# Mean squares with the squares stationary and one moving column, in a one-core decoder step

## The chip, the core and the metric

The kernel runs on one core of a Trainium2 chip. Its engines have a queue each: TensorE (PE; its weight loads are PEld in the profile), VectorE (DVE), ScalarE (ACT), GpSimdE (POOL) and SyncE (SP), which issues the DMAs. They meet at semaphores. The metric is the device time of one execution in microseconds (us); lower is better.

## The reference

One layer of a hybrid decoder for 1088 tokens, 1024 of a prompt and 8 x 8 of a sample. All weights and data are float32.

```
h = rmsnorm(x, norm1_g)                            # D_MODEL = 1024
z = h @ w_in                                       # [c_q 384 | c_kv 256 | k_rope 32 | u 512 | v 512]
c_kv = rmsnorm(c_kv, kv_norm_g); q = rmsnorm(c_q, q_norm_g) @ w_q_up
a = attention(q, c_kv, k_rope) @ w_uv              # 8 heads
g = u * (w_spatial @ layernorm(v) + b)
x = x + [rmsnorm(a, out_norm_mla_g) ; rmsnorm(g, out_norm_gmlp_g)] @ w_out
h2 = rmsnorm(x, norm2_g)
x = x + (silu(h2 @ w_gate) * (h2 @ w_up)) @ w_down
y = rmsnorm(x, final_norm_g)

def rmsnorm(x, g): return x * rsqrt(mean(x * x, axis=-1) + EPS) * g
```

## The kernel before

Activations lie transposed: features on the 128 partitions, tokens along the free dimension. A product in higher precision takes three matmuls, high by high, high by low and low by high part (`mm3`, L871; its three lines L873, L874 and L875 are in most rows of the profile). A mean of squares runs across partitions, so PE computes it.

Five norms go by that route. Their parts are numbered by j: norm 1 over x (`J_N1`, L51) in four parts of 128, 256, 384 and 320 tokens (`CH1`, L49), with 8 row tiles of squares; norm 2 over c_q (3 row tiles) and c_kv (2) in three parts each of 384, 384 and 320 tokens (`CH`, L47); norm 3 over the attention output (4 row tiles), three parts; norm 4 over x after the attention (8 row tiles, which POOL has added up so that two are left), three parts; norm 5 over the output, in another division.

For each part of norms 1 to 4 this happens:

1. ACT squares x (L1429, for norm 4 L1697 too) and counts `nm_sq`.
2. PE sums: `sum_squares` (L877, matmul L881) or, for norm 4, `sum_x2` (L1265, matmul L1271). A 128 x 128 matrix of ones is stationary, the squares move, and every partition of the PSUM bank gets the sum of each token. It counts `nm_sum`.
3. DVE turns this into one value per partition: `columns` (L1892) multiplies each block of 128 tokens by the identity (L1900; for a part of 320 tokens the last 128 go by L1904), adds along the free dimension (L1908) and makes the mean (L1910). It counts `nm_mean`.
4. POOL raises to -0.5 (`power`, L674, L677).
5. DVE builds diagonal matrices of the factors (`diagonals`, L1913, L1919).
6. PE spreads them over the partitions: `spread` (L885, L889), ones times the diagonals.
7. DVE, or ACT and DVE, multiply x by the result.

Norm 5 is summed otherwise, and the change doesn't touch it: `token_sums` (L1352, L1356) has the squares stationary and one column of ones moving, so that each token's sum lands on its own partition, and L2474 makes the mean out of PSUM.

Every engine follows the order in which its block of the program is written. On PE the sums and spreads stand between products: in the first stage, for v (nine token tiles t of 24 matmuls of 512 columns each), the order is sum 0, spread 0, half of t = 0, sum 1, the other half, spread 1, sum 2, t = 1, spread 2, sum 3, t = 2, t = 3, spread 3, t = 4 and so on (L902 to L929). DVE's order there is norm 1 part 0, weight splits, parts 1 and 2, statistics of tiles 0 and 1, part 3, then the statistics and normalisation of the other tiles (L1949 to L1982). SP loads x in four parts and waits for a weight split before the third (L480 to L485). In the stage of c_q and c_kv PE has 18 products of 24 matmuls, with sums and spreads at the places of L986 and L987. In the stage of norm 3 they stand between the samples' scores and products (L1232 to L1262), in that of norm 4 between the last products of `w_out` and the first of the gate (L1275 to L1300).

Of the kernel before, what the change touches and what calls it, by code (L numbers as in the profile page):

```python
# [22 lines left out]
ALU = mybir.AluOpType  # L23
ACT = mybir.ActivationFunctionType
AX = mybir.AxisListType

P = 128
D = 1024
# [16 lines left out]
EPS = 1e-6  # L45
SCALE = QK ** -0.5
CH = [(0, 384), (384, 384), (768, 320)]  # L47
# [6 lines left out]
J_N4 = J_N3 + NC  # L54
# [45 lines left out]
def offsets(n):  # L100

    return [*range(0, n - P + 1, P)] + ([n - P] if n % P else [])
# [28 lines left out]
def build(nc, d):  # L131
    ctx = ExitStack()
    with ctx:
# [14 lines left out]
        small = Region((nc.sbuf_base + 63) // 64 * 64)  # L148
        ident = small.put("ident", [P, P])
        ones = small.put("ones", [P, P])  # L150
        diag = small.put("diag", [P, 3, P])
# [4 lines left out]
        pages = small.put("pages", [1, NB * PAGES], I32)  # L156
        mhalf = small.put("mhalf", [P, 1])
        stat6, mv = small.put("stat6", [P, 2, 6]), small.put("mv", [P, 2, 2])
        sums = small.put("sums", [P, 3])
        ms, rt = small.put("ms", [P, 4, 3]), small.put("rt", [P, 4, 3])  # L160
        ve, rv, ssq = (small.put(n, [P, 4]) for n in ("ve", "rv", "ssq"))
        mx, nmx, sm, rsm = (small.put(n, [P, 4]) for n in ("mx", "nmx", "sm", "rsm"))
# [17 lines left out]
        reg = Region(W0, R0)  # L180
# [5 lines left out]
        reg = Region(W0, R0)  # L186
# [5 lines left out]
        reg = Region(A0, B0)  # L192
        hH, hL = reg.put("hH", [P, KD, T], F32R), reg.put("hL", [P, KD, T], F32R)

        reg = Region(B0, C0)
# [10 lines left out]
        reg = Region(C0, W0)  # L206
# [4 lines left out]
        reg = Region(B0, C0 - 4 * KG * T)  # L211
# [8 lines left out]
        reg = Region(C0, W0)  # L220
# [5 lines left out]
        reg = Region(A0, B0)  # L226
# [11 lines left out]
        reg = Region(rope0, KR0)  # L238
# [8 lines left out]
        reg = Region(B0, PT0)  # L247
# [4 lines left out]
        reg = Region(PT0, PT1)  # L252
# [6 lines left out]
        reg = Region(A0, B0)  # L259
# [4 lines left out]
        reg = Region(B0, C0)  # L264
# [3 lines left out]
        wraw = reg.put("wraw", [P, 4, 1024])  # L268
        reg = Region(B0 + 2 * 16 * HALF * 2, B0 + 3 * 16 * HALF * 2)
        sq2 = reg.put("sq2", [P, 3, T])  # L270
        picked = reg.put("picked", [P, 3, P])
        reg = Region(A0, B0)
        for j in range(3, PROD):
            xH[j], xL[j] = reg.put(f"x{j}H", [P, KH, HALF], F32R), reg.put(f"x{j}L", [P, KH, HALF], F32R)
# [3 lines left out]
        reg = Region(V0, nc.sbuf_usable_end)  # L278
# [5 lines left out]
        reg = Region(B0, C0)  # L284
        ab = [reg.put(f"ab{b}", [P, TURNS, HALF]) for b in range(2)]
        reg = Region(A0, B0)
# [9 lines left out]
        reg = Region(A0 + 4 * TURNS * HALF, A0 + 8 * TURNS * HALF)  # L296
# [4 lines left out]
        reg = Region(V0, V0 + 8192)  # L301
# [3 lines left out]
        ps = ctx.enter_context(nc.psum_tensor("ps", [P, 8, 512], F32))  # L305
# [5 lines left out]
        def sem(name):  # L311
            return ctx.enter_context(nc.semaphore(name))
# [10 lines left out]
            sem(n) for n in ("made", "made_r", "made_z", "sp_masked", "split_seen", "split_hi", "split_lo"))  # L323

        nm_sq, nm_sum, nm_pick, nm_column, nm_mean, nm_pow, nm_diag, nm_spread = (
            sem("nm_" + n) for n in ("sq", "sum", "pick", "column", "mean", "pow", "diag", "spread"))

        n1_x, n1_hi, n1_lo = (sem("n1_" + n) for n in ("x", "hi", "lo"))

# [539 lines left out]
        def _(pe):  # L870
# [6 lines left out]
            def sum_squares(j, bank, sq, k, n):  # L877

                pe.wait_ge(nm_sq, j + 1)
                for kk in range(k):  # L880
                    last = nc.tensor.matmul(ps[:, bank, 0:n], ones[:, :], sq[:, kk, 0:n], start=kk == 0,  # L881
                                            stop=kk == k - 1)
                last.then_inc(nm_sum, 1)

            def spread(j, bank, n):  # L885
# [19 lines left out]
            for t in range(NT):  # L905
# [10 lines left out]
                for k in range(KD):  # L916
# [4 lines left out]
                    if (c := {0: 0, 1: 1, 3: 2, 6: 3}.get(t)) is not None:  # L921

                        pe.wait_ge(n1_lo, KD * c + k + 1)
                    last = mm3(ps[0:m, b, :], hH[:, k, cols], hL[:, k, cols], vwH[:, k, :], vwL[:, k, :],
                               k == 0, k == KD - 1)
# [60 lines left out]
            sums = {9: (0,), 10: (1,), 11: (2,), 15: (3, 4), 16: (5,)}  # L986
# [236 lines left out]
            for u in range(UNITS):  # L1223
                p = u // 4
# [40 lines left out]
            def sum_x2(c):  # L1265

                c0, n = CH[c]
                pe.wait_ge(n4_added, KD - 2)
                pe.wait_ge(nm_sq, J_N4 + c + 1)
                for i in range(2):  # L1270
                    last = nc.tensor.matmul(ps[:, 4 + c, 0:n], ones[:, :], sq2[:, 2 * i, c0:c0 + n],  # L1271
                                            start=i == 0, stop=i == 1)
                last.then_inc(nm_sum, 1)

            for m in range(KD):  # L1275
# [611 lines left out]
        def _(dve):  # L1887
# [1 line left out]

                return nc.vector.scalar_tensor_tensor(out, x, gain, factor, ALU.mult, ALU.mult)  # L1890

            def columns(j, bank, width, n, picked=diag):  # L1892

                full, k = n // P, len(offsets(n))
                dve.wait_ge(nm_sum, j + 1)
                if j:
                    dve.wait_ge(nm_mean, j)
                    if picked is diag:
                        dve.wait_ge(nm_spread, j)
                last = nc.vector.tensor_tensor(picked[:, 0:full, :],  # L1900
                                               ps[:, bank, 0:full * P].rearrange("p (i n) -> p i n", n=P),
                                               ident[:, :].unsqueeze(1).broadcast_to((P, full, P)), ALU.mult)
                if k > full:
                    last = nc.vector.tensor_tensor(picked[:, full, :], ps[:, bank, n - P:n], ident[:, :],  # L1904
                                                   ALU.mult)
                last.then_inc(nm_pick, 1)
                dve.wait_ge(nm_pick, j + 1)
                nc.vector.tensor_reduce(sums[:, 0:k], picked[:, 0:k, :], AX.X, ALU.add).then_inc(nm_column, 1)  # L1908
                dve.wait_ge(nm_column, j + 1)
                nc.vector.tensor_scalar(ms[:, j % 4, 0:k], sums[:, 0:k], 1.0 / width, EPS,  # L1910
                                        ALU.mult, ALU.add).then_inc(nm_mean, 1)

            def diagonals(j, n):  # L1913
# [316 lines left out]

            def columns4(c):

                columns(J_N4 + c, 4 + c, D, CH[c][1], picked)

            def weight_sums(i):
# [418 lines left out]
```

## Time and profile before

| | us |
|---|---|
| three runs, median | 1470.52 |
| lowest and highest of them | 1469.29, 1474.88 |
| the profiled execution | 1473.64 |
| span of the profiled execution | 1471.7 |

| engine | busy us | share of the span | instructions |
|---|---|---|---|
| PE | 1354.1 | 92% | 9216 |
| PEld | 1259.0 | 86% | 9216 |
| DVE | 827.0 | 56% | 1304 |
| ACT | 506.6 | 34% | 870 |
| POOL | 439.4 | 30% | 278 |

### The profile page before, as it was taken

How to read it: one execution, taken by the hardware profiler on the slowest of the kernel's cores; microseconds unless marked ns; L12 is line 12 of the kernel's file. 1: busy time of each engine (PE TensorE's matmuls, PEld its weight loads, DVE VectorE, ACT ScalarE, POOL GpSimd, SP SyncE). 2: the span in 40 equal slices, each digit the busy share in tenths (PEclk: the TensorE clock that was granted, in tenths of full speed). 3: DMA queues.
4: the chain of work that ended last, by engine and by line, in shares of the span. 5: the costliest groups of instructions: out<-in, count | busy, mean ns of one | idle time of the engine just before them, and what ended most of it. 6: DMA issues, size and time to landing. Idle time of an engine off the chain costs nothing.

```text
span 1471.7 us, 23463 instructions
## 1 busy us (share of the span) xinstructions
PE 1354.1 (92%) x9216; PEld 1259.0 (86%) x9216; DVE 827.0 (56%) x1304; ACT 506.6 (34%) x870; POOL 439.4 (30%) x278
## 2 busy tenths in 40 slices
PE   6979998799999898999669999999999989999987
PEld 4758898688888765899659999999999989999987
DVE  4793114666666432514765454434445547989975
ACT  3412212455655431301332222222222224444452
POOL 1161222434333202154644444444444410000000
PEclk9989999899999899999779999999999999999998
DMA  7011010200003532442012222222222249766503
GB/s 230 3 46 59 25 34 4 70 1 19 1 15 117 188 115 112 163 141 94 4 37 74 74 88 80 73 80 76 69 73 73 88 159 368 266 194 229 196 1 122
DMA packets 64376, 142.10 MB, mean 97 GB/s; under 512 B 7490, under 2 KB 14530, under 8 KB 63586
## 3 DMA queue, kind: packets, MB, share of 16 engines
q1 hardware_dynamic: 64290, 140.93, 28.1%
q8 instruction: 57, 0.93, 0.3%
q14 instruction: 29, 0.24, 0.1%
HBM read 118.35 MB, written 22.55 MB: 96 GB/s over the span
## 4 chain that ended last, share of the span: by engine, by line
PE 71%; DVE 15%; issue 4%; DMA 4%; POOL 2%; ACT 2%; SPq 0%; DVEq 0%; POOLq 0%; ACTq 0%
PE ps L873 21%; PE ps L874 21%; PE ps L875 21%; DMA araw<-in_w_dn 2%; PE ps L1096 2%; PE ps L881 2%; DVE x L1890 2%; PE ps L1159 1%; DVE aHL L2442 1%; DMA x<-in_x 1%; DVE bHL L2445 1%; PE ps L1202 1%; DVE mx L2113 1%; DVE bsum L2434 1%; DVE mL L2227 1%
## 5 line engine op out<-in xcount | busy, mean ns | idle before, releaser
L827 POOL TENSOR_TENSOR ws<-wraw,ws 128x1024 fp32r<-128x1024 f32 x55 | 136.5, 2483 | 199.9 <-ACT ws L1425 199.9
L873 PE MATMUL ps<-bHL,aHL 128*128 128x272 f32 x616 | 180.2, 293 | 11.5 <-DVE bHL L2445 11.5
L875 PE MATMUL ps<-bHL,aHL 128*128 128x272 f32 x616 | 179.0, 291 | 0.0
L874 PE MATMUL ps<-bHL,aHL 128*128 128x272 f32 x616 | 178.8, 290 | 0.0
L873 PEld LDWEIGHTS ps<-bHL,aHL 128*128 128x128 f32 x616 | 117.8, 191 | 13.0 <-DVE bHL L2445 13.0
L2308 DVE TENSOR_TENSOR bufP<-bufP,ps 128x544 f32<-128x544 f32 x66 | 47.5, 721 | 139.3 <-PE ps L875 137.1
L1425 ACT ACTIVATE ws<-wraw 128x1024 fp32r<-128x1024 f32 x55 | 58.3, 1061 | 181.9 <-PE ps L875 181.9
L874 PEld LDWEIGHTS ps<-bHL,aHL 128*128 128x128 f32 x616 | 117.8, 191 | 0.0
L875 PEld LDWEIGHTS ps<-bHL,aHL 128*128 128x128 f32 x616 | 117.6, 191 | 0.0
L827 POOL TENSOR_TENSOR ws<-wsum,ws 128x1024 fp32r<-128x1024 f32 x22 | 64.8, 2946 | 66.2 <-ACT ws L1425 66.2
L865 POOL TENSOR_TENSOR rt<-ms,mhalf 128x3 f32<-128x3 f32 (+1 forms) x3 | 3.1, 1039 | 265.3 <-DVE ms L2474 265.3
L2129 DVE TENSOR_TENSOR pTL<-ps,pTH 128x512 fp32r<-128x512 f32 (+1 forms) x96 | 53.1, 554 | 46.3 <-ACT pTH L1425 44.8
L782 POOL TENSOR_TENSOR prob<-prob,rsm 128x128 f32<-128x128 f32 (+5 forms) x48 | 49.7, 1042 | 96.7 <-DVE rsm L2102 96.7
L2308 DVE TENSOR_TENSOR bufC<-bufP,ps 128x544 f32<-128x544 f32 x42 | 30.3, 720 | 80.3 <-PE ps L875 72.9
L1425 ACT ACTIVATE aHL<-araw 128x512 fp32r<-128x512 f32 x66 | 41.7, 631 | 89.1 <-DVE araw L2417 59.9
L1425 ACT ACTIVATE pTH<-ps 128x512 fp32r<-128x512 f32 (+1 forms) x96 | 46.9, 490 | 52.1 <-PE ps L1096 51.1
L1096 PE MATMUL ps<-ident,prob 128*128 128x128 f32 x288 | 54.2, 295 | 11.5 <-DVE prob L2107 7.4
L873 PE MATMUL ps<-x4H,ws 128*128 128x272 f32 x176 | 52.3, 297 | 7.4 <-POOL x4L L832 7.4
L873 PE MATMUL ps<-x3H,ws 128*128 128x272 f32 x176 | 51.8, 294 | 6.9 <-DVE x3L L2278 6.9
L1578 ACT ACTIVATE prob<-ps,nmx 128x128 f32<-128x128 f32 (+3 forms) x64 | 47.4, 741 | 28.9 <-DVE nmx L2116 28.9
L873 PE MATMUL ps<-x1H,ws 128*128 128x272 f32 x176 | 52.2, 297 | 5.2 <-POOL x1L L832 5.2
L2113 DVE TENSOR_REDUCE mx<-ps 128x1 f32<-128x128 f32 (+3 forms) x64 | 48.1, 751 | 12.5 <-PE ps L1077 12.2
(356 smaller groups left out, 4509.9 us busy)
## 6 DMA issues: line engine op xcount, KB each, us to landing
araw<-in_w_dn SPq DMA_DIRECT2D x121, 256.0 KB, 3.3
wraw<-in_w_gu SPq DMA_DIRECT2D x44, 512.0 KB, 3.6
cp<-in_cache SPq DMA_DIRECT2D x64, 272.0 KB, 4.7
ab<-acts SPq DMA_DIRECT2D x34, 272.0 KB, 4.9
acts<-bufC SPq DMA_DIRECT2D x22, 272.0 KB, 2.1
x<-in_x SPq DMA_DIRECT2D x4, 1088.0 KB, 8.1
x2s<-x SPq DMA_DIRECT2D x8, 544.0 KB, 9.2
x<-x2s SPq DMA_DIRECT2D x8, 544.0 KB, 6.2
```

Of the source, the lines that this page charges most:

```text
L782: pool.tensor_tensor(row, row, rsm[:, r % 4:r % 4 + 1].broadcast_to((P, n)), ALU.mult).then_inc(s_pn, 1)
L827: pool.tensor_tensor(w[:, 1, :], w_source(j), w[:, 0, :], ALU.subtract).then_inc(cw_lo, 1)
L873: nc.tensor.matmul(out, wh, xh, start=start, stop=False)
L874: nc.tensor.matmul(out, wh, xl, start=False, stop=False)
L875: return nc.tensor.matmul(out, wl, xh, start=False, stop=stop)
L881: last = nc.tensor.matmul(ps[:, bank, 0:n], ones[:, :], sq[:, kk, 0:n], start=kk == 0, stop=kk == k - 1)
L1096: last = nc.tensor.transpose(ps[:, 4 + x % 2, P * qi:P * qi + P], prob[:, at:at + P], ident[:, :])
L1425: return nc.scalar.activation(out, x, ACT.Copy, scale=scale)
L1578: nc.scalar.activation(prob[:, prob_at(qt):prob_at(qt) + n], psf[:, 1024 * (r % 2):1024 * (r % 2) + n], ACT.Exp, bias=nmx[:, s:s + 1], sca ...
L2113: nc.vector.tensor_reduce(mx[:, s], psf[:, at:at + P * (qt + 1)], AX.X, ALU.max).then_inc(s_mx, 1)
L2129: nc.vector.tensor_tensor(pTL[:, x % 4, c0:512], ps[:, 4 + x % 2, c0:512], pTH[:, x % 4, c0:512], ALU.subtract).then_inc(t_free, 1)
L2308: nc.vector.tensor_tensor(halves(out[:, g, :]), halves(x[:, g, :]), pair(b + 2 * g), ALU.add).then_inc(added, 1)
```

## The change

The sums of norms 1 to 4 take the form of norm 5. The squares of 128 tokens are the stationary operand and one column of ones moves; for each block of 128 tokens the row tiles accumulate in one PSUM column, 500 + i of the same bank. A part of 320 or 384 tokens needs three blocks, and the last block of a part of 320 overlaps the one ahead. DVE's pick and reduction go, and the mean is read out of PSUM. `columns` waits only for the sum and, so that the ring of four slots in `ms` isn't overwritten, for an earlier power; the waits for the last mean and the last spread go. The small buffers `sums` and `picked` go too.

```diff
             def sum_squares(j, bank, sq, k, n):
 
                 pe.wait_ge(nm_sq, j + 1)
-                for kk in range(k):
-                    last = nc.tensor.matmul(ps[:, bank, 0:n], ones[:, :], sq[:, kk, 0:n], start=kk == 0,
-                                            stop=kk == k - 1)
+                for i, o in enumerate(offsets(n)):
+                    for kk in range(k):
+                        last = nc.tensor.matmul(ps[:, bank, 500 + i:501 + i], sq[:, kk, o:o + P], ones[:, 0:1],
+                                                start=kk == 0, stop=kk == k - 1)
                 last.then_inc(nm_sum, 1)
...
-                for i in range(2):
-                    last = nc.tensor.matmul(ps[:, 4 + c, 0:n], ones[:, :], sq2[:, 2 * i, c0:c0 + n],
-                                            start=i == 0, stop=i == 1)
+                for i, o in enumerate(offsets(n)):
+                    for x in range(2):
+                        last = nc.tensor.matmul(ps[:, 4 + c, 500 + i:501 + i], sq2[:, 2 * x, c0 + o:c0 + o + P],
+                                                ones[:, 0:1], start=x == 0, stop=x == 1)
                 last.then_inc(nm_sum, 1)
...
-            def columns(j, bank, width, n, picked=diag):
-
-                full, k = n // P, len(offsets(n))
+            def columns(j, bank, width, n):
+
+                k = len(offsets(n))
                 dve.wait_ge(nm_sum, j + 1)
-                if j:
-                    dve.wait_ge(nm_mean, j)
-                    if picked is diag:
-                        dve.wait_ge(nm_spread, j)
-                last = nc.vector.tensor_tensor(picked[:, 0:full, :],
-                                               ps[:, bank, 0:full * P].rearrange("p (i n) -> p i n", n=P),
-                                               ident[:, :].unsqueeze(1).broadcast_to((P, full, P)), ALU.mult)
-                if k > full:
-                    last = nc.vector.tensor_tensor(picked[:, full, :], ps[:, bank, n - P:n], ident[:, :],
-                                                   ALU.mult)
-                last.then_inc(nm_pick, 1)
-                dve.wait_ge(nm_pick, j + 1)
-                nc.vector.tensor_reduce(sums[:, 0:k], picked[:, 0:k, :], AX.X, ALU.add).then_inc(nm_column, 1)
-                dve.wait_ge(nm_column, j + 1)
-                nc.vector.tensor_scalar(ms[:, j % 4, 0:k], sums[:, 0:k], 1.0 / width, EPS,
+                if j >= 4:
+                    dve.wait_ge(nm_pow, j - 3)
+                nc.vector.tensor_scalar(ms[:, j % 4, 0:k], ps[:, bank, 500:500 + k], 1.0 / width, EPS,
                                         ALU.mult, ALU.add).then_inc(nm_mean, 1)
```

PE's order in the first stage, around the sum of norm 1's part 3 (L881 before, L880 after; L889 and L888 are the spread of part 2), before:

```order
L875 MATMUL ps<-vwH,hL 128x512
L889 MATMUL ps<-diag,ones 128x128 [waits nm_diag]
L889 MATMUL ps<-diag,ones 128x128 x2
L881 MATMUL ps<-sq_96,ones 128x320 [waits nm_sq]
L881 MATMUL ps<-sq_96,ones 128x320 x7
L873 MATMUL ps<-vwH,hH 128x512
```

And after:

```order
L873 MATMUL ps<-vwH,hL 128x512
L888 MATMUL ps<-diag,ones 128x128 [waits nm_diag]
L888 MATMUL ps<-diag,ones 128x128 x2
L880 MATMUL ps<-ones,sq_95 128x1 [waits nm_sq]
L880 MATMUL ps<-ones,sq_95 128x1 x23
L871 MATMUL ps<-vwH,hH 128x512
```

The sum stands where it stood; 8 matmuls of 320 moving columns have become 24 of one.

DVE's order in norm 4, from the end of part 0 to the scaling behind part 1 (`x_146` is x after the attention), before:

```order
L2262 TENSOR_TENSOR x_146<-x_146,ps 128x320 [waits w_ready]
L1900 TENSOR_TENSOR picked<-ps,ident 128x384 [waits nm_mean,nm_sum]
L1908 TENSOR_REDUCE sums<-picked 128x3 [waits nm_pick]
L1910 TENSOR_SCALAR ms<-sums 128x3 [waits nm_column]
L1919 TENSOR_TENSOR diag<-ident,rt 128x384 [waits nm_spread,nm_pow]
L1890 SCALAR_TENSOR_TENSOR x_146<-x_146,g_57,rs 128x272 [waits x2_out0,rs_x] x2
```

And after:

```order
L1907 TENSOR_TENSOR diag<-ident,rt 128x384 [waits nm_spread,nm_pow]
L2250 TENSOR_TENSOR x_145<-x_145,ps 128x320 [waits w_ready]
L1898 TENSOR_SCALAR ms<-ps 128x3 [waits nm_pow,nm_sum]
L1907 TENSOR_TENSOR diag<-ident,rt 128x384 [waits nm_spread,nm_pow]
L1890 SCALAR_TENSOR_TENSOR x_145<-x_145,g_57,rs 128x272 [waits x2_out0,rs_x] x2
```

The pick (L1900) and the reduction (L1908) are gone, and nothing else has changed places.

## Rows read from the trace of the kernel before

**Rows 1.** The page, part 4: the chain that ended last, by engine.
```profile
PE 71%; DVE 15%; issue 4%; DMA 4%; POOL 2%; ACT 2%; SPq 0%; DVEq 0%; POOLq 0%; ACTq 0%
```
**Rows 2.** Timeline of PE: start us, us, instruction, [idle before <- releaser].
```profile
1429.26 1.28 PE L1356 MATMUL ps<-ones,sqh 128*128 128x1 f32 x10 [2.47 <-DVE sqh L2467]
1430.39 0.37 PE L873 MATMUL ps<-bHL,aHL 128*128 128x272 f32 x1
```
**Rows 3.** The chain in order of time: start us, us on the chain, what.
```profile
206.08 1.94 PE ps L881 x6
...
218.97 1.62 PE ps L881 x6
...
36.62 0.23 PE ps L873
...
105.26 0.43 PE ps L875
```
**Rows 4.** Instructions of lines L1900 and L1908: duration ns min/median/max, first and last start.
```profile
L1900 DVE TENSOR_TENSOR diag<-ps,ident x13: 283/541/558, 10.9 to 593.5; 128x384 f32<-128x384 f32 x7, 128x256 f32<-128x256 f32 x5, 128x128 f32<-128x128 f32 x1
...
L1908 DVE TENSOR_REDUCE sums<-diag x13: 286/553/554, 11.3 to 594.2; 128x3 f32<-128x384 f32 x11, 128x1 f32<-128x128 f32 x1, 128x2 f32<-128x256 f32 x1
```
**Rows 5.** Timeline of all engines, norm 1 part 0.
```profile
10.95 0.28 DVE L1900 TENSOR_TENSOR diag<-ps,ident 128x128 f32<-128x128 f32 x1
...
11.59 0.15 DVE L1910 TENSOR_SCALAR ms<-sums 128x1 f32<-128x1 f32 x1
```
**Rows 6.** Instructions of line L2474, norm 5's mean out of PSUM.
```profile
L2474 DVE TENSOR_SCALAR ms<-ps x3: 152/155/161, 1432.0 to 1461.5; 128x3 f32<-128x3 f32 x2, 128x5 f32<-128x5 f32 x1
```
**Rows 7.** By stretch: us, busy (instructions) PE, PEld, DVE, ACT, POOL; PEclk, DMA, GB/s.
```profile
1417.70:1421.10 3.40, 1.78 (x12) 1.55 (x12) 3.37 (x6) 3.09 (x4) 0.00 (x0) 1.00 0.01 2
...
1427.90:1431.30 3.40, 2.04 (x17) 2.04 (x18) 3.37 (x7) 0.00 (x0) 0.00 (x0) 1.00 0.00 0
1431.30:1434.70 3.40, 3.40 (x17) 3.40 (x16) 2.01 (x5) 0.43 (x1) 1.17 (x1) 0.50 0.00 0
1434.70:1438.10 3.40, 3.40 (x31) 3.40 (x30) 0.44 (x1) 1.11 (x3) 0.00 (x0) 1.00 0.00 0
```
**Rows 8.** By stretch, elsewhere.
```profile
246.90:253.70 6.80, 4.99 (x16) 4.21 (x17) 3.03 (x8) 0.84 (x1) 0.85 (x1) 0.50 0.00 0
...
506.30:516.50 10.20, 8.61 (x39) 4.73 (x38) 0.08 (x1) 4.41 (x9) 0.00 (x0) 0.50 0.80 301
...
588.20:595.00 6.80, 6.17 (x14) 4.60 (x15) 3.55 (x8) 6.80 (x14) 0.01 (x1) 0.50 0.00 0
...
58.00:102.00 44.00, 34.55 (x146) 26.14 (x146) 40.61 (x58) 11.87 (x24) 26.06 (x21) 0.94 0.11 36
```
**Rows 9.** Timeline of PE, norm 1: sum of part 1, spread of part 3.
```profile
22.90 4.67 PE L881 MATMUL ps<-sq,ones 128*128 128x256 f32 x16
27.22 0.58 PE L873 MATMUL ps<-vwH,hH 128*128 128x512 f32 x1
...
59.55 0.94 PE L889 MATMUL ps<-diag,ones 128*128 128x128 f32 x6 [1.55 <-DVE diag L1919]
```
**Rows 10.** Timeline of PEld: the loads of norm 1's first sum, at half clock.
```profile
6.51 3.49 PEld L881 LDWEIGHTS ps<-sq,ones 128*128 128x128 f32 x16 [6.51 <-issue]
```
**Rows 11.** Timelines of PE and DVE, the last two parts of norm 2.
```profile
248.71 1.65 PE L889 MATMUL ps<-diag,ones 128*128 128x128 f32 x6 [4.01 <-DVE diag L1919]
...
252.53 0.42 DVE L1900 TENSOR_TENSOR diag<-ps,ident 128x256 f32<-128x256 f32 x1 [0.99 <-PE ps L881]
```
**Rows 12.** The chain in order of time, last sum of norm 3.
```profile
588.83 4.65 PE ps L881 x8
```
**Rows 13.** Timelines of PE and POOL, norm 4 and the first splits behind it.
```profile
698.96 0.94 PE L889 MATMUL ps<-diag,ones 128*128 128x128 f32 x6 [1.21 <-DVE diag L1919]
705.26 1.65 PE L889 MATMUL ps<-diag,ones 128*128 128x128 f32 x6 [5.37 <-DVE diag L1919]
...
707.78 4.72 POOL L832 TENSOR_TENSOR x0L<-x,x0H 128x272 fp32r<-128x272 f32 x4 [3.16 <-ACT x0H L1425]
```

More of the change, by code:

```diff
@@ L158, in build @@
         stat6, mv = small.put("stat6", [P, 2, 6]), small.put("mv", [P, 2, 2])
-        sums = small.put("sums", [P, 3])
         ms, rt = small.put("ms", [P, 4, 3]), small.put("rt", [P, 4, 3])
@@ L270, in build @@
         sq2 = reg.put("sq2", [P, 3, T])
-        picked = reg.put("picked", [P, 3, P])
         reg = Region(A0, B0)
@@ L323, in build @@
             sem(n) for n in ("made", "made_r", "made_z", "sp_masked", "split_seen", "split_hi", "split_lo"))
-        nm_sq, nm_sum, nm_pick, nm_column, nm_mean, nm_pow, nm_diag, nm_spread = (
-            sem("nm_" + n) for n in ("sq", "sum", "pick", "column", "mean", "pow", "diag", "spread"))
+        nm_sq, nm_sum, nm_mean, nm_pow, nm_diag, nm_spread = (
+            sem("nm_" + n) for n in ("sq", "sum", "mean", "pow", "diag", "spread"))
         n1_x, n1_hi, n1_lo = (sem("n1_" + n) for n in ("x", "hi", "lo"))
@@ L2231, in columns4 @@
             def columns4(c):
-                columns(J_N4 + c, 4 + c, D, CH[c][1], picked)
+                columns(J_N4 + c, 4 + c, D, CH[c][1])
             def weight_sums(i):
```

## The prediction, on record before the changed kernel ran

> **What bounds the kernel now.** I read the page first. Its chain of waits puts 71% on PE and 15% on DVE [rows 1], so time on either counts only where that engine arrives last. I then looked at each of the 16 norms of the first four kinds (here called n1, n2, n3 and n4, with parts counted from 0) and asked of its sum, its picking and its spread which one is late. In most of them the spread stands in PE's order behind other matmuls, and the picking on DVE is done by then. PE really waits for DVE at six: the first and last part of n1, the middle part of n2 (the last one is behind DVE's later work), the last part of n3, the last two of n4.
>
> **What one new matmul costs.** The trace of before has the new form already: the fifth norm sums 128 x 128 squares against one column. Ten of its records start at 1429.26 and PE's next work at 1430.39, so one takes 0.113 us [rows 2]. Every float32 matmul shows as two records (five such matmuls are these ten). A full sum costs by its moving columns: six records of 384 columns take 1.94 us, 0.323 each; six of 320 take 1.62 us, 0.27 each [rows 3]. For one row tile of squares that is before 2 x 0.323 = 0.65 us (384) or 0.54 us (320), after, three blocks of 128, 6 x 0.112 = 0.67 us. So at full clock the new sum gains PE nothing: +0.025 us a tile at 384, +0.13 us at 320, about 0 at 256 and 128. Over n1 (8 tiles), n2 (3 and 2), n3 (4) and n4 (2) this makes +3.4 us of PE time, 1.1 us of it in the last part of n1.
>
> The row shows 0.113 us although one column moves. The Trainium skill, page "TensorE: Matmul & The Clock Gate", section "Back-to-back issue gap", gives about 60 cycles (25 ns) for 1 to 64 columns; by that alone the 342 new records would take 30 us less than by the row. Its section on loading the stationary operand gives the number of columns over 1.2, that is 107 ns for 128, and with that the trace agrees.
>
> **What DVE loses.** Pick and reduce: 0.54 + 0.55 us [rows 4] and two gaps of 0.04, 1.17 us for a part of 384. In the first part, of 128, they stand between 10.95 and 11.59: 0.64 us, the pick alone 0.28 [rows 5]. A part of 320 picks twice (0.42 for 256 columns, and those 0.28 again, overlapping a little): 1.25 us. The mean stays and reads PSUM at 0.155 us [rows 6] where it took 0.17.
>
> **The clock.** Here I expect the change to lose. Two stretches beside each other [rows 7]: in 1417.7 to 1421.1 PE is busy for 1.78 us with full matmuls, and the clock stays at 2.4 GHz. In 1427.9 to 1431.3 it is busy for 2.04 us, 1.13 of them with the one-column sum, and right behind it the granted clock is 0.50 (1.2 GHz). The idle gap ahead was 2.47 us [rows 2], against 2.17 in the first stretch, so it is not proof. But taken as idle, the one-column sum explains it; taken as work, it does not. I read: PE with one moving column keeps no clock. The half-clock stretch behind that sum lasts 3.4 us, two behind long waits 6.8 us [rows 7, 8]; matmuls of full width ran before the clock came back. A stretch costs half its length: 1.7 or 3.4 us where PE is late.
>
> The same page, section "What's actually happening", says that the clock follows how busy PE has been. Taken by PE's busy row, which is full during these sums, that rule would keep the clock: the first rival below.
>
> **Start (n1).** The first norm is 0.64 us earlier, and with it the weight split on DVE and the load of x that waits behind it: -0.64. The sum of part 1 starts at half clock, as all before it, and the clock rises within it: 22.90 to 27.22, 4.3 us [rows 9]. Records bound by the load take about 0.21 us at half clock: 16 in 3.49 us, the end of the last one included [rows 10]. If the clock cannot rise in it: 32 x 0.21 = 6.7 us, +2.4; and the 12 matmuls behind it run at 0.43 instead of 0.23 us [rows 3], +2.4. The sum of part 2: 48 x 0.112 = 5.4 us for 16 x 0.323 = 5.2, +0.2; it is nothing but one column, so the clock falls in it or at its end, and the 24 matmuls behind pay: +3.4. Part 3: 5.4 for 16 x 0.27 = 4.3, +1.1, and +3.4 again. PE came free for the last spread at 59.55 - 1.55 = 58.0 [rows 9]; now at 58.0 - 0.64 + 2.4 + 2.4 + 0.2 + 3.4 + 1.1 + 3.4 = 70.3. DVE's 1.25 us there are then hidden. Spread 3: **+10.7 us** against 59.55. Queued behind it on DVE are the scaling and all v tiles; DVE is busy 40.6 of the next 44 us [rows 8], so nothing is caught up. Bounds: without any clock loss -0.9 (58.0 - 0.64 + 0.2 + 1.1 = 58.6); with stretches of 10.2 us, such as granted behind the small matmuls at 506.3 [rows 8], two times +1.7 more. I take the 6.8 us of the two long waits.
>
> **n2.** PE-bound through parts 0 to 3: sums +0.54 and +0.1. Then PE idles 4.01 us for the spread of part 4 [rows 11]: DVE's 1.17 go from the path. The last sum runs at half clock, 12 x 0.21 for 4 x 0.54 (twice 0.27) us: +0.35. The last pick starts after a wait for it [rows 11]: -1.25. DVE's order behind is dense, so it keeps this. Parts 3 and 4 are summed back to back, 2.7 us of one column; if the clock falls there it costs 1.7, I take +1.0 (0 to 3.4). Sum **-0.4**.
>
> **n3.** Two sums of 24 records lie on PE's path: +0.1 each, for 2.7 us each (24 x 0.112) at one column, amid small matmuls. Clock: +2.4 (0 to 6.8). Their picks are hidden: PE reaches the spread as late as DVE. Part 2 is at half clock: 24 x 0.21 and its tail of 0.2 against 4.65 us [rows 12], +0.6; then DVE's picking ahead of the product, -1.25. Sum **+2.0**.
>
> **n4.** PE idles 1.21 and 5.37 us for DVE, and POOL starts its splits 3.16 us late [rows 13]; POOL and DVE then set the pace for 50 us. -1.17 and -1.25, sums +0.08; the sums of parts 1 and 2 with a spread between may drop the clock before the spread of part 1: +0.7 (0 to 1.7). Sum **-1.6**. From the first turn of gate and up on nothing changes.
>
> **Total**: 10.7 - 0.4 + 2.0 - 1.6 = +10.7 us. The profiled execution took 1473.64 us (span 1471.7 and 1.9 around it), so 1484.3; the median of the runs, 1470.52, lies 3.1 below it: **1481.2 us**.
>
> **Rivals.**
> - The clock takes a one-column sum for work. Then n1 gives -0.9, n2 -1.4, n3 +0.2 + 0.6 - 1.25 = -0.45, n4 -2.34: -5.1, **1465.4**. For it: PE's busy row is full. Against: rows 7. It decides at the sum of part 2 in n1: if its 48 records keep 0.112 us and the matmuls behind them 0.23, this is the case.
> - Short stretches: the clock falls, but the half-clock stretches are of 3.4 us, as behind the fifth norm [rows 7], and it still rises within the sum of part 1 thanks to the matmuls ahead of it. n1: 58.0 - 0.64 + 1.2 + 0.2 + 1.7 + 1.1 + 1.7 = 63.3, +3.7, and n3 +1: -0.4 + 1.0 + 3.7 - 1.6 = +2.7, up to +5: **1475**.
> - More is lost: stretches of 10.2 us in n1, two in n3: +3.4 + 4, **1488.5**.
> - Every pick and reduce counts, 18 us, with no loss on PE: **1452**. The spreads that stand in PE's order without a wait speak against it.
>
> **Chances.** Forecast 0.60, short stretches 0.19, clock kept 0.13, more lost 0.06, all picks 0.02. What differs by under 0.5% (7.4 us) this measurement can hardly tell from no change. Above 1477.9 lie the forecast but for a little, the worst case and a part of the short stretches: slower 0.67; 0.27 within; faster 0.06. The likeliest case's own range is 1476 to 1487; the range given reaches down to most of the short stretches and leaves out the clock-kept case.
>
> **What would show it.** The sum of part 1 in 6.7 us; granted clock 0.5 right after the sums of parts 2 and 3 in n1; spread 3 near 70 instead of 59.55, with no PE wait for the diagonal ahead of it; the first u tile near 112. After n4 PE's idle 5.37 shrinks to some 4. Wrong if the matmuls behind the 48 records take 0.23 us, or if DVE makes up the lag before the u tiles.

## The result, and the profile after

| kernel | median of its runs | runs | ratio to before | 95% interval |
|---|---|---|---|---|
| before | 1472.68 us (1469.29 to 1478.12) | 21 | | |
| after | 1480.24 us | 21 | 1.0047 | 1.0036 to 1.0057 |

The changed kernel is slower by 7.6 us, and the interval excludes no change. Twenty of its runs lie between 1472.3 and 1484.3 us; the other one, 1557.8 us at a granted clock of 0.82, was a slow one and is left out of the ratio. The forecast was 1481.2. Its profiled execution took 1483.91 us (span 1482.0), 10.3 us more than that of before (1473.64, span 1471.7).

The page of after, part 1: busy time, share of the span and instructions of each engine; then the first row of part 4, the chain by engine.

```profile
PE 1375.1 (93%) x9428; PEld 1291.7 (87%) x9428; DVE 810.9 (55%) x1267; ACT 506.6 (34%) x870; POOL 439.5 (30%) x278
...
PE 74%; DVE 13%; issue 4%; DMA 3%; POOL 2%; ACT 2%; SPq 0%; DVEq 0%; POOLq 0%; ACTq 0%
```

The chain has moved from DVE to PE: 74 and 13% where it was 71 and 15% [rows 1]. DVE lost the picking, and the path did not get shorter by it.

The timeline of PE in after, norm 1: start us, us, instruction, idle time before it in brackets.

```profile
22.62 6.82 PE L880 MATMUL ps<-ones,sq 128*128 128x1 f32 x32
29.30 0.77 PE L871 MATMUL ps<-vwH,hH 128*128 128x512 f32 x1
...
34.57 0.79 PE L888 MATMUL ps<-diag,ones 128*128 128x128 f32 x4
35.20 7.35 PE L880 MATMUL ps<-ones,sq 128*128 128x1 f32 x48
42.41 0.77 PE L871 MATMUL ps<-vwH,hH 128*128 128x512 f32 x1
...
51.52 6.67 PE L880 MATMUL ps<-ones,sq 128*128 128x1 f32 x48
58.04 0.77 PE L871 MATMUL ps<-vwH,hH 128*128 128x512 f32 x1
...
71.01 0.83 PE L888 MATMUL ps<-diag,ones 128*128 128x128 f32 x6
```

These answer to [rows 9]. The sum of part 1 takes 29.30 - 22.62 = 6.7 us where it took 4.3. The spread of part 3 stands at 71.01 where it stood at 59.55, and its row has no bracket: PE no longer waits for the diagonal, it is late by itself.

The stretches of after in norm 1: us, busy (instructions) of PE, PEld, DVE, ACT, POOL, then the granted clock.

```profile
34.60:38.40 3.80, 3.80 (x35) 3.80 (x33) 2.91 (x8) 1.64 (x4) 0.00 (x0) 1.00 0.61 236
38.40:48.60 10.20, 10.20 (x35) 8.85 (x36) 3.90 (x11) 4.00 (x5) 0.85 (x1) 0.50 0.00 1
52.00:55.40 3.40, 3.40 (x33) 3.40 (x32) 3.34 (x8) 1.94 (x4) 0.00 (x0) 1.00 0.00 0
55.40:62.30 6.90, 6.90 (x24) 6.03 (x24) 5.32 (x12) 4.62 (x8) 0.00 (x0) 0.51 0.01 2
```

And the same time in before:

```profile
34.60:38.40 3.80, 3.80 (x16) 2.66 (x15) 3.58 (x10) 2.89 (x4) 0.00 (x0) 1.00 0.66 257
38.40:48.60 10.20, 10.20 (x47) 8.00 (x46) 6.36 (x14) 3.78 (x7) 0.85 (x1) 1.00 0.00 1
```

PE is busy without a gap in both. In after the clock is 1.00 from 34.6 to 38.40, although nearly all of that is one-column matmuls; then it is 0.50, still within the sum, for 10.2 us, and from within the next sum for 6.9. In before it is 1.00 in both stretches. Behind the fall the full matmuls start 0.43 us apart in after (42.98 to 48.53) and 0.23 in before.

The clock column has a limit at the start of a run: it shows 1.00 for the time before the first change on record. The distances between starts show the clock there. In after the 32 records from 22.62 on are 0.21 us apart and the full matmuls behind them 0.43, which is half clock; within the spread at 34.57 the distance falls from 0.21 to 0.11. In before it falls at 25.03, within the sum of part 1. So after's clock came up some 10 us later than before's, and was full for only 3.4 us before it fell again at 38.4.

How late after is against before, at places that both kernels have (the forecasts of the prediction beside them):

| place | before | after | lag | change of the lag: measured, forecast |
|---|---|---|---|---|
| norm 1, scaling behind its last spread (DVE) | 60.52 | 71.88 | 11.36 | +11.4, +10.7 |
| second half of the first u tile (PE) | 101.48 | 112.84 | 11.36 | 0, 0 |
| norm 2, first sum (PE) | 205.92 | 216.00 | 10.08 | -1.3, 0 |
| norm 2, low part of the latents (DVE) | 256.23 | 266.08 | 9.85 | -0.2, -0.4 |
| norm 3, low part of mL ahead of the product (DVE) | 596.35 | 609.03 | 12.68 | +2.8, +2.0 |
| norm 4, first split (POOL) | 707.78 | 718.10 | 10.32 | -2.4, -1.6 |
| last instruction | 1471.7 | 1482.0 | 10.3 | 0, 0 |

Between norms 1 and 2, where the change has nothing, 1.3 us come back, at two half-clock stretches that fall otherwise on the same work. Some 0.7 us come back at the end of the stretch of 10.2 us that both have in the u tiles (from 96.7 in before, from 106.6 in after, the lag then 10.7), and 0.6 at one that is 6.8 us long in before (from 161.6) and 3.4 in after (from 174.9).

### The profile page after: what moved, and what is told of

Same layout as the page of the kernel before. It is cut to its first block, busy times and chain, and to the rows that moved or that the text cites. A ratio compares the mean times of both kernels' runs of the same rounds, so it can differ in the third digit from the quotient of the medians.

```text
span 1482.0 us, 23847 instructions
## 1 busy us (share of the span) xinstructions
PE 1375.1 (93%) x9428; PEld 1291.7 (87%) x9428; DVE 810.9 (55%) x1267; ACT 506.6 (34%) x870; POOL 439.5 (30%) x278
## 4 chain that ended last, share of the span: by engine, by line
PE 74%; DVE 13%; issue 4%; DMA 3%; POOL 2%; ACT 2%; SPq 0%; DVEq 0%; POOLq 0%; ACTq 0%
PE ps L871 22%; PE ps L872 21%; PE ps L873 21%; PE ps L880 3%; DMA araw<-in_w_dn 2%; PE ps L1095 2%; DVE x L1890 1%; PE ps L1201 1%; PE ps L1158 1%; DVE aHL L2430 1%; DVE bHL L2433 1%; DVE mx L2101 1%; DVE mL L2215 1%; DVE x L2443 1%; DVE vf L1967 1%
```

## The experiments

Each ratio is to runs of before on the same chip: median 1472.64 of 19 runs for e1_wide to e4_part2_one, 1472.95 of 20 for e5_norm5 to e8_wide_pick on another chip, and 1473.12 (one run) for e9_after_again. All results:

| run | what it is | median us | ratio to before, 95% interval |
|---|---|---|---|
| after | one column everywhere, no picking | 1480.24 | 1.0047 (1.0036 to 1.0057) |
| e1_wide | 128 columns, no picking | 1466.10 | 0.9953 (0.9937 to 0.9969) |
| e2_full_nopick | full sums, no picking (wrong factors) | 1462.60 | 0.9926 (0.9905 to 0.9947) |
| e3_n1_full | norm 1 as before, the others as after | 1473.04 | 0.9993 (0.9978 to 1.0009) |
| e4_part2_one | e1_wide, one sum of norm 1 with one column | 1473.73 (one) | |
| e5_norm5 | e1_wide, norm 5 widened too | 1467.34 | 0.9964 (0.9950 to 0.9978) |
| e6_n1_one | e1_wide, norm 1 with one column | 1476.56 | 1.0036 (1.0023 to 1.0049) |
| e7_n3_one | e1_wide, norm 3 with one column | 1467.74 | 0.9965 (0.9952 to 0.9978) |
| e8_wide_pick | 128 columns, picking kept | 1474.52 | 1.0007 (0.9994 to 1.0020) |
| e9_after_again | after, profiled again | 1480.39 (one) | |

My theory: behind matmuls with one moving column TensorE's clock falls as it does behind idle time. Its main rival: the clock falls because the stationary operand is changed for every matmul, or because the pace is set by that load.

### e1_wide: the same loads, 128 moving columns

```diff
-    matmul(ps[:, bank, 500 + i:501 + i], sq[:, kk, o:o + P], ones[:, 0:1], ...)
+    matmul(ps[:, bank, o:o + P], sq[:, kk, o:o + P], ones[:, :], ...)
...
-    tensor_scalar(ms[:, j % 4, 0:k], ps[:, bank, 500:500 + k], ...)
+    tensor_scalar(ms[:, j % 4, 0:k], ps[:, bank, 0:P * k - P + 1:P], ...)
```

The same in norm 4's sum. All 128 columns of a block hold the same numbers, so the third block of a part of 320 may overlap the second.

> Squares stationary as in the changed kernel, the same number of weight loads, but 128 moving columns of ones in place of one; DVE's mean reads every 128th column. Clock theory (few moving columns leave the array idle): records keep 0.11 us, the granted clock stays 1.00 behind the sums of parts 2 and 3 of the first norm, the last spread there starts at 58.5 to 59.5 us, and the median is 5 to 7 us below the kernel before, 1466 to 1468. Rival (the clock falls because the stationary operand is changed for every matmul, or because the pace is that of the load): same loads, so still 0.50 there, the spread near 71, and about 1480. Rival (the clock had nothing to do with it, 128 columns just cost more): above 1480.

Measured: 1466.10, 14 us below after and 6.5 below before. The timeline of PE in e1_wide:

```profile
22.86 4.78 PE L880 MATMUL ps<-ones,sq 128*128 128x128 f32 x32
...
32.63 5.63 PE L880 MATMUL ps<-ones,sq 128*128 128x128 f32 x48 [1.80 <-ACT sq L1429]
...
44.25 5.52 PE L880 MATMUL ps<-ones,sq 128*128 128x128 f32 x48
60.54 0.83 PE L888 MATMUL ps<-diag,ones 128*128 128x128 f32 x6
```

Its stretches, of and behind the two sums of 48:

```profile
32.60:38.20 5.60, 5.57 (x49) 5.57 (x50) 5.14 (x14) 3.10 (x8) 0.00 (x0) 1.00 0.87 327
38.20:41.60 3.40, 3.40 (x17) 2.78 (x16) 0.80 (x3) 2.34 (x1) 0.85 (x1) 1.00 0.02 8
44.20:49.70 5.50, 5.50 (x51) 5.50 (x51) 5.19 (x11) 2.62 (x5) 0.00 (x0) 1.00 0.01 3
49.70:53.10 3.40, 3.40 (x17) 2.77 (x16) 3.04 (x7) 2.39 (x4) 0.00 (x0) 1.00 0.00 0
```

As many loads (50 and 51), PE as busy, the time of a sum as short as one column's at full clock (48 x 0.112 = 5.4 us): and the clock stays 1.00 behind both. The sum of part 1 starts at half clock in both kernels; here its records go from 0.21 us apart to 0.11 at 24.98, as before's clock came up at 25.03, and with one column none of the 32 does. Number and pace of the loads are excluded; what is left is how many columns move. The spread of part 3 came 1 us later than expected (60.54): the squares of part 2 began 1.44 us later in this execution (29.81 against 28.37 us, both waiting for the transfer of x), so PE waited 1.80 us for them.

### e2_full_nopick: DVE's side of the change alone

```diff
-    for i, o in enumerate(offsets(n)):
-        for kk in range(k):
-            matmul(ps[:, bank, 500 + i:501 + i], sq[:, kk, o:o + P], ones[:, 0:1], ...)
+    for kk in range(k):
+        matmul(ps[:, bank, 0:n], ones[:, :], sq[:, kk, 0:n], ...)
...
-    tensor_scalar(ms[:, j % 4, 0:k], ps[:, bank, 500:500 + k], ...)
+    tensor_scalar(ms[:, j % 4, 0:k], ps[:, bank, 0:k], ...)
```

> Full sums with the ones stationary as in the kernel before, but DVE takes no diagonal: it reads the first columns of the sum as if they were the means (the picking is left out, so the scale factors are those of other tokens). DVE's part of the change alone. Clock theory: no one-column sums, so clock as before; spread of the last part of the first norm at 57.5 to 58.5, total 6 to 8 us below before, 1465 to 1467. Rival (what DVE saves is hidden, only the PE side counts): within 2 us of before, 1471 to 1474. Rival (all 18 us of DVE count): about 1455.

Measured: 1462.60, 10 us below before (by the interval of the ratio 8 to 14), more than the 6 to 8 expected: of the 18 us that DVE saves, some 10 reach the time. The spread was not at 57.5 to 58.5 but at 63.76, and this profiled execution is the slowest of the six (1467.79 us). Its timeline of PE, and the stretches ahead of the fall of its clock and behind:

```profile
34.95 7.12 PE L879 MATMUL ps<-sq,ones 128*128 128x384 f32 x16 [3.16 <-ACT sq L1427]
```

```profile
29.50:36.30 6.80, 3.64 (x17) 2.63 (x16) 2.36 (x6) 3.59 (x4) 0.22 (x1) 1.00 1.03 280
36.30:39.80 3.50, 3.50 (x7) 1.92 (x6) 3.50 (x11) 1.95 (x6) 0.00 (x0) 0.51 0.80 306
```

PE waited 3.16 us for the squares of part 2 (0.34 in before), and the clock fell within the full sum behind it. So full sums are no insurance against a wait; but this stretch ends after 3.5 us, in the same sum.

### e8_wide_pick: PE's side of it alone, with the clock kept

The sums of e1_wide in the kernel before, and with them the function that picks and reduces on DVE taken over from before unchanged.

> The PE side of the 128-column run alone: squares stationary, 128 moving columns, and DVE still picks the diagonal and reduces it as before. PE's sums take 3.4 us more in all and the clock stays, so 0 to 3 us above before: 1473 to 1476; the DVE side is then worth 7 to 9 us against the 128-column run. If the clock were lost by the number of loads, 1484 and more.

Measured: 1474.52, 1.6 us above before, an interval that includes no change, and far from the 1484 of a clock lost by the number of loads. e1_wide, which drops the picking from it, is 8.4 us lower, so DVE's side measures 8.4 us here and 10.0 in e2_full_nopick. The two sides alone add to -10.0 + 1.6 = -8.4 us, and both together (e1_wide) give -6.5. The three intervals are 2 to 3 us wide on either side, so that this difference of 2 us shows nothing.

### e3_n1_full: norm 1 as before

```diff
+    for kk in range(k if j < 4 else 0):
+        matmul(ps[:, bank, 0:n], ones[:, :], sq[:, kk, 0:n], ...)
-    for i, o in enumerate(offsets(n)):
+    for i, o in enumerate(offsets(n) if j >= 4 else ()):
```

and for these four parts DVE picks and reduces as before.

> First norm as in the kernel before (full sums, picking on DVE), the other three norms with one column. If the 11.4 us that the two traces differ by after the first norm are all its own: 11 us below the changed kernel, 1468 to 1470, and 3 to 4 below before. Rival (the loss moves: a first norm that ends earlier finds the next engine no more ready, and u tiles or weights hold it): 1473 to 1478.

Measured: 1473.04. By the profiles the first half of the expectation holds: span 1471.1, 10.9 below after. By the medians it missed: 7.2 below after, not 11, and no difference from before where 3 to 4 us were expected. The median lies at the low edge of the rival's range, but nothing holds the gain up behind norm 1: against before the profiled execution is 0.9 us early at the last spread of norm 1 (58.67 for 59.55) and 0.8 us early ahead of norm 2. In the other three norms one column and no picking about cancel: in its profile norm 3 loses 2.8 us and norm 4 gains 2.4, as in after. Why 11 became 7 is the question of the last run.

### e6_n1_one and e4_part2_one: one column in norm 1 alone, in one sum alone

```diff
+    w = 1 if j < J_N2 else P          # e4_part2_one: 1 if j == J_N1 + 2
-    matmul(ps[:, bank, o:o + P], sq[:, kk, o:o + P], ones[:, :], ...)
+    matmul(ps[:, bank, a:a + w], sq[:, kk, o:o + P], ones[:, 0:w], ...)
```

Here a is o where w is 128, and P * i where it is 1 (o in e4_part2_one, where a part of 384 makes both the same).

> As the 128-column run, but all four sums of the first norm have one moving column. Theory that the clock's loss in the first norm is the whole of what the change loses there: spread of the last part at 70 to 72 us instead of 60.5, and a median 7 to 11 us above the 128-column run, 1473 to 1477. Rival (part of the changed kernel's loss of 14 us against the 128-column run is elsewhere in equal measure, so that the first norm makes only half): 1470 to 1472.

> As the run with 128 columns, but the sum of part 2 of the first norm alone has one moving column. Clock theory: the granted clock is 0.50 for 6.8 to 10.2 us from within or right behind that sum, and nowhere else in the first 90 us that the 128-column run does not have it; last spread of the first norm 3.4 to 5.1 us later than there. Theory that the number of loads or the sum's time counts: no difference from the 128-column run.

Measured: e6_n1_one 1476.56, 10.5 us above e1_wide, the spread of part 3 at 70.69. Norm 1's one column costs 10.5 us by the medians, within the expected 7 to 11 (12 by the two ratios, each to its own chip). Its profiled execution, 1472.69, is the fastest of six: it is 10.2 us late at that spread, and 5.7 at the end (spans 1470.9 and 1465.2), since three later half-clock stretches (near 594, 1208 and 1420) fall otherwise than in e1_wide. Three stretches of e6_n1_one, then three of e4_part2_one, with the sum that they belong to:

```profile
30.00:37.80 7.80, 7.80 (x43) 6.80 (x42) 3.06 (x8) 3.65 (x5) 0.50 (x1) 1.00 0.90 302
37.80:48.00 10.20, 10.20 (x36) 8.98 (x36) 4.16 (x12) 4.23 (x6) 0.85 (x1) 0.50 0.00 1
54.80:61.60 6.80, 6.80 (x26) 6.03 (x26) 5.26 (x11) 4.87 (x8) 0.00 (x0) 0.50 0.01 2
```

```profile
30.53 9.11 PE L881 MATMUL ps<-ones,sq 128*128 128x1 f32 x48 [2.67 <-ACT sq L1430]
...
28.60:32.00 3.40, 1.47 (x13) 1.47 (x14) 1.36 (x5) 2.82 (x4) 0.00 (x0) 1.00 1.11 239
32.00:45.60 13.60, 13.60 (x51) 12.27 (x51) 4.75 (x13) 4.51 (x7) 0.85 (x1) 0.50 0.34 127
45.60:49.00 3.40, 3.40 (x21) 2.94 (x20) 0.19 (x1) 0.00 (x0) 0.00 (x0) 0.99 0.00 0
```

In e6_n1_one the places of after come back. In e4_part2_one the last spread came 4.4 us later than in e1_wide (64.91 against 60.54), within the expected 3.4 to 5.1; a stretch of 13.6 us was not expected. PE had waited 2.67 us for the squares right ahead of the sum, and the clock fell at 32.00, 1.5 us into it: 13 of its 48 records start about 0.11 us apart, the other 35 0.21. The clock came back only at 45.6, 6 us into the full matmuls behind.

e1_wide waited only 1.80 us there, so that this pair differs in two things. e5_norm5 (below), whose norm 1 is that of e1_wide, happened to wait 2.74 us and tells them apart:

```profile
32.49 7.25 PE L880 MATMUL ps<-ones,sq 128*128 128x128 f32 x48 [2.74 <-ACT sq L1430]
...
33.30:36.60 3.30, 3.30 (x18) 3.30 (x17) 3.30 (x10) 1.74 (x5) 0.00 (x0) 0.50 1.06 403
36.70:40.00 3.30, 3.30 (x29) 3.26 (x29) 1.45 (x5) 0.82 (x3) 0.00 (x0) 1.00 0.09 34
```

The clock falls behind this wait too, at 33.3, with 128 columns moving; but it is back after 3.4 us, in the same sum. From the sum's start to the last spread of norm 1 it takes 27.9 us in e1_wide, 29.5 in e5_norm5 and 34.4 in e4_part2_one. By these single executions the longer wait costs 1.6 us and the one column 4.8. e7_n3_one, whose norm 1 has 128 columns as well, waited 3.04 us and took 29.5.

### e7_n3_one: one column in norm 3 alone

The same edit with J_N3 <= j < J_N4.

> As the 128-column run, but the three sums of the third norm (24 records each) have one moving column. Clock theory: half-clock stretches of 3.4 to 6.8 us behind the sums of its parts 0 and 1, the product's end 2.5 to 3.5 us later, median 1468.5 to 1470. Rival (amid small matmuls and waits the clock's loss is hidden): 1466.

Measured: 1467.74, 1.6 us above e1_wide by the medians and 0.8 below the expected 1468.5 to 1470; the intervals of the two ratios overlap, so that the median alone doesn't show a loss. The stretches do:

```profile
532.20:535.60 3.40, 3.40 (x31) 3.27 (x30) 1.37 (x4) 0.60 (x1) 0.00 (x0) 1.00 0.00 0
535.60:542.50 6.90, 6.90 (x31) 4.61 (x32) 1.89 (x5) 2.63 (x3) 0.86 (x1) 0.51 0.01 2
542.50:545.90 3.40, 3.40 (x32) 2.61 (x28) 0.00 (x0) 0.47 (x1) 0.00 (x0) 1.00 0.16 21
...
556.10:559.50 3.40, 3.34 (x8) 1.11 (x10) 0.00 (x0) 0.00 (x0) 0.00 (x0) 0.50 1.05 420
```

A half-clock stretch of 6.9 us begins within the first sum (533.99 to 537.6 in its timeline), where e1_wide has none; after has it too, at 550.4. It is there in all four profiled executions with one column in norm 3 (these two, e3_n1_full and e9_after_again) and in none of the other seven. Against e1_wide it costs 3.1 us. The stretch at 556.1 costs 1.7 more, but it isn't the sum's: ahead of it PE waits 1.94 us for DVE in every run, and the clock falls there in seven of the eleven profiled executions, e2_full_nopick, e4_part2_one and e8_wide_pick among them, whose norm 3 has full or 128-column sums. The last sum and the product behind it give 1.5 us back. The end of the product comes 3.2 us later than in e1_wide, as expected (2.5 to 3.5), and 1.7 of it is that draw.

### e5_norm5: norm 5 widened as well

```diff
+    w = (512 - SUB) // len(offsets(n))
-    matmul(ps[:, bank + gap * i, 500 + i:501 + i], src[:, o:o + P], ones[:, 0:1], ...)
+    matmul(ps[:, bank, SUB + w * i:SUB + w * i + w], src[:, o:o + P], ones[:, 0:w], ...)
```

The last part has 128 columns at the end of three banks. In the first two parts the mean reads the first column of each block; in the last it still reads column 500, which lies in the block and holds the same number.

> As the 128-column run, and the fifth norm's sums widened as well, into the free columns of their banks: 48, 80 and 128 moving columns in its three parts. If the one-column sum of its first part is what takes the clock there (half-clock stretch of 3.4 us in before, 6.8 in the changed kernel): 1 to 2 us below the 128-column run, 1464 to 1465. If the wait of about 2.5 us ahead of that sum takes it: no difference, 1466.

Measured: 1467.34, no gain over e1_wide. In e1_wide the clock is 0.50 from 1421.1 on, and the sum starts at 1421.4: PE's wait of 2.5 us ahead of it has taken the clock before the first record. In e5_norm5 itself the clock still falls, at 1422.5, 0.6 us into the sum with 48 columns, behind a wait of 2.10 us; and it falls at 1412.2, among full matmuls behind a wait of 2.21 us, where before kept it behind 2.17. With it falls the weight that I gave to [rows 7]: there too the wait alone may be the cause. The stretch at the sum is of 3.4 us with 48 columns and of 6.8 in e1_wide, where one column moves.

### e9_after_again: the changed kernel, a second profile

> The changed kernel as it is, for a second profile, since its first profiled execution is 3.7 us above the median of its runs while the kernel before's is 1 us above its own. If the clock's stretches fall differently from execution to execution, this one shows a last spread of the first norm between 67 and 72 us and differs from the first in the stretches' places or lengths; if not, 71 us and the same stretches, and the difference lies outside the norms.

Measured: span 1478.7, 3.3 less than in the first profile. Norm 1 is the same: last spread at 71.48, half clock from 38.5 to 48.7 and from 55.5. The difference comes in norm 2. There, in e9_after_again:

```profile
249.70:256.50 6.80, 6.01 (x40) 5.82 (x39) 1.73 (x5) 0.00 (x0) 0.85 (x1) 1.00 0.00 0
```

and in the first profile of after:

```profile
250.00:256.80 6.80, 6.80 (x24) 6.80 (x24) 0.56 (x1) 0.00 (x0) 0.77 (x1) 0.50 0.00 0
```

Both have the 24 one-column records of parts 3 and 4 just ahead (from 247.77 and 248.04). Once the clock fell at 250.0, within the last of them, once it did not, and in 6.8 us PE gets through 24 or 40 instructions. The second execution is 0.3 us late ahead of this place and 2.9 early behind it (285.34 for 288.25 at one matmul), so that 3.2 us arise here; what differs later adds up to 0.4. The same program thus has executions some 3.3 us apart by whether one sum costs the clock or not. The expectation was half wrong: the stretches do differ, but in norm 2, not in norm 1.

It can be a part of why after's runs reach from 1472.3 to 1484.3 us, and why medians and single profiles of e3_n1_full and after differ by different amounts (7.2 and 10.9; against the second profile of after it is 7.6). Each run's mean granted clock is on record: 0.946 to 0.948 in the eight slowest of these twenty, 0.950 to 0.952 in the three fastest, though 0.951 stands at 1480.2 and 1480.5 too. An estimate from these: 0.004 of 1480 us is 6 us of lost clock, half of the range. Where the stretches lay in the other runs is not recorded.

## Why the prediction was right

**The clock.** Right, and the step on which the sign hung. "PE with one moving column keeps no clock" was read from two stretches that I called no proof, and e5_norm5 shows that they were none. The proof is e1_wide: 128 columns, the same loads at the same pace, and 14 us come back; e6_n1_one takes 10.5 of them away again in norm 1 alone. The rival "the clock takes a one-column sum for work" gave 1465.4, or 5.1 us below before; e1_wide, which is that case made real, measures 1466.10, 6.5 below a before whose median had been taken 2 us too low. By the same page of the Trainium skill, "TensorE: Matmul & The Clock Gate", section "What's actually happening", the clock follows how busy PE has been; the trace agrees only if busy is not the profile's busy row, which is 3.80 of 3.80 us ahead of the fall at 38.4.

**Norm 1**, forecast +10.7, measured +11.4. By its terms, each from the starts in the timelines of both kernels:

| term | forecast | measured |
|---|---|---|
| ahead of the sum of part 1 | -0.64 | -0.28 |
| sum of part 1 at half clock | +2.4 | 6.68 - 4.32 = +2.36 |
| the 12 matmuls behind it | +2.4 | 5.27 - 2.94 = +2.33 |
| spread of part 1, PE's wait of 0.34 before sum 2 | 0 | -0.40 |
| part 2: its sum, and the 24 matmuls behind | +0.2, +3.4 | +2.24, +2.66 |
| part 3: its sum, and the 48 matmuls behind | +1.1, +3.4 | +2.46, +1.64 |
| PE's wait for the last diagonal | -1.55 | -1.55 |

The last step of norm 1, the first row of the table above, is +11.46 by the spread (71.01 - 59.55). What failed is where the half clock falls: "the clock falls in it or at its end, and the 24 matmuls behind pay". It fell inside both sums, so these pay part of it, and the first stretch was of 10.2 us, not 6.8. The prediction's instance of 10.2 us, at 506.3 [rows 8], is itself one of 13.7: the row ends within it. Part 2 thus costs 4.9 for 3.6, part 3 4.1 for 4.5. At the start the first spread was 0.95 us earlier (12.95 for 13.90), but the matmuls ahead of the sum wait for DVE's split of the weights, and that came only 0.3 us earlier.

**Norm 2**, forecast -0.4, measured -0.2, and the nearness is luck. The sums (+0.57 for +0.54) came as forecast, and PE's idle time ahead of the spread of part 4 went from 4.01 to 2.83 us (-1.18 for -1.17). The clock cost 3.2 us in the first profile, and nothing in the second: the forecast's +1.0 (0 to 3.4) is a mean of two cases, and no execution has it. Behind the spread of part 4 after gains 2.9, not 0.9 (1.25 less the 0.35 for a last sum at half clock): before is at half clock there until 253.7 [rows 8], after is not, and its 12 records took 1.4 us where 2.5 were forecast. In the second profile norm 2 is -3.2.

**Norm 3**, forecast +2.0, measured +2.8, again of two errors. To the end of the scores after loses 4.75 us where sums and clock were forecast at +2.6: 3.3 at the stretch of 6.8 us from within the first sum, and 1.5 at one of 3.4 us from 570.9, which falls behind the wait of 1.94 us for DVE and isn't the sum's (e7_n3_one). The last sum, forecast 0.6 longer, held DVE up 0.7 less than before's: the clock fell at 605.0, 1.5 us into it, where in before it had fallen at 588.2, ahead of the sum. It took 3.93 us rather than the forecast 5.2, and the product behind it paid for that instead. The picking gave its 1.25.

**Norm 4**, forecast -1.6, measured -2.4: both pickings count in full (1.17 + 1.25). I had taken off 0.7 for the clock, and the half-clock stretch at 710.8 to 721.0 is as long as that of before at 700.9 to 711.1: the sums took nothing more. The timeline of PE in after:

```profile
708.62 0.91 PE L888 MATMUL ps<-diag,ones 128*128 128x128 f32 x6
709.37 1.40 PE L1271 MATMUL ps<-ones,sq 128*128 128x1 f32 x12
710.62 1.49 PE L888 MATMUL ps<-diag,ones 128*128 128x128 f32 x6
715.59 1.65 PE L888 MATMUL ps<-diag,ones 128*128 128x128 f32 x6 [3.47 <-DVE diag L1907]
```

The idle 1.21 and 5.37 us of [rows 13] are 0 and 3.47.

**From profile to median**, the step that was right by luck. The forecast took 3.1 us off because before's profiled execution lay that far above the median of 3 runs; with 21 runs it is 1.0. And after's profiled execution lies 3.7 above its own median. Against its profile the change costs 10.3 us (forecast 10.7), against the medians 7.6. The two errors cancel in 1481.2, and one of them is in part the stretch in norm 2 that some executions have. The prediction also called a difference under 0.5% hardly measurable and gave "slower" beyond that 0.67; the ratio, 0.47%, lies just inside that band, and with 21 runs on either side it was clear of no change.

**DVE's side** is not shown to be off. The clock-kept rival has -5.1, PE's longer sums already in it; e1_wide has -6.5, with an interval of 4.6 to 9.3. Without PE's part, e2_full_nopick gives 10 where 6 to 8 was expected, and e8_wide_pick against e1_wide 8.4.

## What to carry to other kernels

When a sum over partitions is only wanted per row, putting the data on the stationary side removes the picking of a diagonal, but give it as many moving columns as the load of the stationary operand hides anyway: here 128 columns take the time of one, keep the clock where PE doesn't wait long ahead of them (behind waits of 2.74 and 3.04 us it fell, for 3.4 us), and turn a kernel 7.6 us slower than before into one 6.5 us faster. The loss does not show in the busy share: PE's busy row is full during the sum, and it is the end of the sum and the full matmuls behind it that run at half clock, so read the granted clock by stretches, not the busy share. And where an edit acts through the clock, one profile is one draw; take a second before a term of 3 us is believed.

## What was not expected of the hardware

- 128 moving columns of float32 take the time of one beside a stationary operand of 128 columns: in e1_wide 48 records take 5.28 us to the next matmul's start (44.25 to 49.53), 0.110 each, against 0.113 [rows 2]. At half clock a record takes 0.21 us with either.
- While one-column sums ran at half clock, the clock did not come back: not in the 6.7 us of part 1 in norm 1 (32 records), where full matmuls (4.3 us) and 128 columns (4.5 us) let it rise, and not in the 7.5 us of e4_part2_one, where the stretch lasted 13.6 us against 3.4 with 128 columns behind a like wait (e5_norm5).
- The same wait does not always take the clock: behind a wait of 1.94 us for DVE in norm 3, the same in every run, it fell in seven profiled executions and stayed in four. Two executions of one program differ by 3.3 us, nearly all of it through one stretch of the clock.
